# Attention scores of a head in two segments, three and two PSUM banks, instead of three

## The chip, the cores and the metric

The kernel runs on one core of a Trainium2 chip. The metric is the device time of one launch in microseconds (us). The kernel before takes 3364.94 us, the median of three runs (3364.42 to 3366.22).

## The reference, cut to what matters

The reference is one step of a backbone whose layer has attention, retention and routed experts. The change touches the attention alone:

```python
def block_attention(q, k, v):          # 2048 latent tokens in blocks of 128, 8 query heads, 2 key/value heads
    ...
    def one_block(qblk):
        s = jnp.einsum('bkgqd,bskd->bkgqs', qblk, k).astype(jnp.float32) * scale
        p = jax.nn.softmax(s, axis=-1).astype(v.dtype)
        return jnp.einsum('bkgqs,bskd->bkgqd', p, v)
```

A latent query sees 2048 latent keys and 128 cached context keys, 2176 keys or 17 key tiles of 128. The 128 new context tokens see only their own 128 keys. A head has 64 dimensions.

## The kernel before, in words

The stage `attention` runs over query tiles i = 0 to 16 (NT = 16): sixteen latent tiles, then one of context tokens. A tile has 8 heads h, and each head is one step. Tiles 2 to 14 are one hardware loop; the 8 steps of a tile are written out in it.

The work of a step is software-pipelined over heads. In step h TensorE (PE) turns the probabilities of head h (`turn`, L1292: transposes of 128x128 blocks with the identity, 4 in one PSUM bank; turns 0 to 3 have 4 blocks, turn 4 has one), multiplies values for the pair of heads before (`value`, L1310), and computes the scores of head h + 2 (`scores`, L1282). ScalarE (ACT) takes the exponentials of head h + 1 (`exp`, L1419, which also sums its outputs and reads that sum out) and keeps the high part of each turned bank (`turn`, L1427). VectorE (DVE) takes the maxima over the scores of head h + 2 (`scores`, L1502), combines them and scales them (L1506, L1512: `nm`, the bias of the exponential), keeps the low part of each turned bank (`turn`, L1529) and so frees the bank, and sums and inverts the totals (`total`, L1519, L1521).

The scores of a head fill five PSUM banks, `ps_s`; of these there is one set. So each segment of scores of head h + 2 waits until the exponential of the same segment of head h + 1 has read it: `pe.wait_ge(exped[seg], n)` in `scores`. The first turn of a head waits until its last exponential is done. The turns go through two further banks, `ps_t`, in rotation with the folds of a value pair (`fold`, L1322, every even step), the turned queries (`q`, L1263, at the head of step 6), the turned outputs (`out`, L1343, behind step 3) and a piece of a modulation vector (`mod`, L1331, in the place of the fold in steps 5 and 7).

Each engine executes its instructions in the order of the program, and that order is written by hand, one list for each engine: `PE_STEP`, `ACT_STEP`, `DVE_STEP`. `BANK_W` holds the columns of each score bank, `SEGS` the (first bank, banks) of each segment, `SEG_ORDER` the order of the segments. Before, segment 0 is 2 banks of 448 columns, segment 1 the same, segment 2 one bank of 384. The context tile has one segment of 128 columns and only turn 4.

Of the kernel before, what the change touches and what calls it, by code (L numbers as in the profile page):

```python
# [6 lines left out]
P = 128  # L7
# [3 lines left out]
NT = T_LAT // P  # L11
# [4 lines left out]
NQ = 8  # L16
# [29 lines left out]
AX = mybir.AxisListType.X  # L46
# [500 lines left out]
def retention(nc, g, a, s):  # L547

    with ExitStack() as ctx:
# [364 lines left out]
        def _(pe):  # L914
# [95 lines left out]

KEY_TILES = NT + 1

BANK_W = [448, 448, 448, 448, KEY_TILES * P - 4 * 448]
SEGS = [(0, 2), (2, 2), (4, 1)]
CTX_KEYS = NT + 1


PE_STEP = [("turn", 0), ("turn", 1), ("value", 0), ("value", 1), ("turn", 2), ("turn", 3), ("scores", 0), ("value", 2),
           ("scores", 2), ("turn", 4), ("fold", 0), ("scores", 1)]
ACT_STEP = [("keep", 0), ("turn", 0), ("turn", 1), ("exp", 0), ("exp", 2), ("turn", 2), ("turn", 3), ("exp", 1),  # L1020
            ("turn", 4)]
DVE_STEP = [("turn", 0), ("turn", 1), ("total", 0), ("turn", 2), ("turn", 3), ("scores", 0), ("turn", 4), ("scores", 2),
            ("fold", 0), ("scores", 1)]
SEG_ORDER = [0, 2, 1]
PIECES = [(0, 3), (3, 6), (6, 9), (9, 12), (12, 15), (15, KEY_TILES)]
GROUP = 2
NGRP = NQ // GROUP
# [2 lines left out]
def attention(nc, g, a, s):  # L1030


    with ExitStack() as ctx:
        k = Core(nc, ctx)
# [14 lines left out]
        fold = k.sb("a_fold", [P, HD])  # L1049
        o_sum = k.sb("a_o_sum", [P, GROUP, P])  # L1050
        att = k.sb("a_att", [P, NQ, HD])
        mx, nm = k.sb("a_mx", [P, 2, 4]), k.sb("a_nm", [P, 2])
        sums, total_s, rsum = k.sb("a_sums", [P, 2, 3]), k.sb("a_total", [P, 2]), k.sb("a_rsum", [P, NQ])
        attT = k.sb("a_attT", [P, 4, P])
        HALF = P // 2
        wm = [k.sb(f"a_wm{i}", [P, DC, w]) for i, w in enumerate((P, HALF))]
# [1 line left out]
        ps_s = k.ps("a_ps_s", [P, 5, 512])  # L1058
# [3 lines left out]
        kv_in, k_hi_ok, k_lo_ok, vals_ok = k.sems("a_kv_in", 2), k.sem("a_k_hi_ok"), k.sem("a_k_lo_ok"), k.sem("a_vals_ok")  # L1062
        k_turned, k_kept = k.sem("a_k_turned"), k.sem("a_k_kept")
        q_in, q_hi_ok, q_lo_ok = k.sem("a_q_in"), k.sem("a_q_hi_ok"), k.sem("a_q_lo_ok")
        scored, exped = k.sems("a_scored", 3), k.sems("a_exped", 3)
        max_ok, max_all, nmax_ok = k.sem("a_max_ok"), k.sem("a_max_all"), k.sem("a_nmax_ok")
        sum_ok, rsum_ok, hi_kept = k.sem("a_sum_ok"), k.sem("a_rsum_ok"), k.sem("a_hi_kept")
        filled, emptied = k.sems("a_filled", 2), k.sems("a_emptied", 2)
# [8 lines left out]
        block = blocks.enter_context(nc.Block())  # L1077

        def segs_of(i):
            return [2] if isinstance(i, int) and i == NT else SEG_ORDER  # L1080

        def turns_of(i):
            return [4] if isinstance(i, int) and i == NT else [0, 1, 2, 3, 4]

        def seg_scores(seg, w=None):
            b, m = SEGS[seg]
            return ps_s[:, b:b + m, 0:w or BANK_W[b]]

        def seg_probs(i, h, seg):
            b, m = SEGS[seg]  # L1090
            if isinstance(i, int) and i == NT:
                return prob[h % 2][:, (KEY_TILES - 1) * P:].rearrange("p (b w) -> p b w", b=1)
            at = sum(BANK_W[0:b])
            return prob[h % 2][:, at:at + m * BANK_W[b]].rearrange("p (b w) -> p b w", b=m)

        def seg_width(i, seg):
            return P if isinstance(i, int) and i == NT else BANK_W[SEGS[seg][0]]

# [138 lines left out]
        def _(pe):  # L1237
# [30 lines left out]
            def scores(i, h, seg, q_uses):  # L1268

                n = i * NQ + h  # L1270
                ctx_tile = isinstance(i, int) and i == NT
                if seg == segs_of(i)[0] and h == 0:
                    for b in range(2):
                        pe.wait_ge(emptied[b], q_uses[b])
                if not (isinstance(n, int) and n == 0):
                    pe.wait_ge(exped[seg], n)
                first, m = SEGS[seg]
                for b in range(first, first + m):
                    w = seg_width(i, seg)
                    src = CTX_KEYS * P if ctx_tile else sum(BANK_W[0:b])  # L1280
                    for part in range(2):
                        ins = nc.tensor.matmul(ps_s[:, b, 0:w], qT[:, h, :], keys[:, part, h // QPK, src:src + w],  # L1282
                                               start=(part == 0), stop=(part == 1))
                ins.then_inc(scored[seg], 1)
# [65 lines left out]
            for h in range(2):  # L1350
                for seg in SEG_ORDER:
                    scores(0, h, seg, [1, 1])
# [32 lines left out]
        def _(act):  # L1385
# [19 lines left out]
            def queries_hi(i):  # L1405
                act.wait_ge(q_in, (i + 1) * 16)
                if not (isinstance(i, int) and i == 0):

                    act.wait_ge(scored[2], (i - 1) * NQ + 1)
                nc.scalar.activation(q_parts[:, :, 0, :], q_row[:, :, :], ACT.Copy).then_inc(q_hi_ok, 1)  # L1410

            def exps(i, h, seg):

                n = i * NQ + h
                if seg == segs_of(i)[0]:
                    act.wait_ge(nmax_ok, n + 1)
                    if not (isinstance(n, int) and n < 2):
                        act.wait_ge(sum_ok, n - 1)
                nc.scalar.activation(seg_probs(i, h, seg), seg_scores(seg, seg_width(i, seg)), ACT.Exp,  # L1419
                                     bias=nm[:, h % 2:h % 2 + 1], scale=scale,  # L1420
                                     accum_out=sums[:, h % 2, seg:seg + 1]).then_inc(exped[seg], 1)

            def leave(i, h, kind, n, b, before):
                if kind == "turn":
                    act.wait_ge(filled[b], before + 1)
                    out = pT_hi[h // 2 % 2][:, 4 * n:min(4 * n + 4, KEY_TILES), h % 2, :]
                    nc.scalar.activation(out, ps_t[b][:, 0:out.shape[1], :], ACT.Copy).then_inc(hi_kept, 1)  # L1427
                elif kind == "q":
                    act.wait_ge(filled[b], before + 1)
                    nc.scalar.activation(qT[:, n * 4:n * 4 + 4, :], ps_t[b][:, :, :], ACT.Copy).then_inc(emptied[b], 1)  # L1430
                elif kind == "out":
                    act.wait_ge(filled[b], before + 1)
                    if n == 0 and not (isinstance(i, int) and i == 1):
                        act.wait_ge(att_out, (i - 1) * 16)
                    nc.scalar.activation(attT[:, 2 * n:2 * n + 2, :], ps_t[b][:, 0:2, :], ACT.Copy).then_inc(emptied[b], 1)

            def keep_sums(t, grp):
                act.wait_ge(valued, group_index(t, grp) + 1)
                nc.scalar.activation(o_sum[:, :, :], ps_o[:, :, :], ACT.Copy).then_inc(o_kept, 1)

            queries_hi(0)
            start = Bank(-1)
            for half_at in range(2):
                leave(0, 0, "q", half_at, *start.next())
            for seg in SEG_ORDER:
                exps(0, 0, seg)

            def body(i):
                last_tile = isinstance(i, int) and i == NT
                bank = Bank(i)  # L1450
                for h in range(NQ):
                    bank_of = bank.step(i, h)
                    for kind, n in step_events(i, h, ACT_STEP):
                        if kind == "exp":
# [19 lines left out]
        def _(dve):  # L1474
# [23 lines left out]
            def maxima(i, h, seg):  # L1498

                n = i * NQ + h  # L1500
                dve.wait_ge(scored[seg], n + 1)
                nc.vector.tensor_reduce(mx[:, h % 2, seg:seg + 1], seg_scores(seg, seg_width(i, seg)), AXY, ALU.max)\  # L1502
                    .then_inc(max_ok, 1)
                if seg == segs_of(i)[-1]:
                    dve.wait_ge(max_ok, (n + 1) * 3 if not (isinstance(i, int) and i == NT) else NT * NQ * 3 + h + 1)
                    nc.vector.reduce_max(mx[:, h % 2, 3:4], mx[:, h % 2, min(segs_of(i)):3], AX).then_inc(max_all, 1)  # L1506
                    dve.wait_ge(max_all, n + 1)
                    if not (isinstance(n, int) and n < 2):
                        dve.wait_ge(exped[SEG_ORDER[-1]], min(n - 1, NT * NQ) if isinstance(n, int) else n - 1)
                        if isinstance(n, int) and n - 1 > NT * NQ:  # L1510
                            dve.wait_ge(exped[2], n - 1)
                    nc.vector.tensor_scalar(nm[:, h % 2:h % 2 + 1], mx[:, h % 2, 3:4], -scale, None, ALU.mult)\  # L1512
                        .then_inc(nmax_ok, 1)

            def total(i, h):

                n = i * NQ + h
                dve.wait_ge(exped[segs_of(i)[-1]], n + 1)
                nc.vector.reduce_sum(total_s[:, h % 2:h % 2 + 1], sums[:, h % 2, min(segs_of(i)):3], AX).then_inc(sum_ok, 1)  # L1519
                dve.wait_ge(sum_ok, n + 1)  # L1520
                nc.vector.reciprocal(rsum[:, h:h + 1], total_s[:, h % 2:h % 2 + 1]).then_inc(rsum_ok, 1)  # L1521

# [54 lines left out]
            def body(i):  # L1577
                last_tile = isinstance(i, int) and i == NT
                bank = Bank(i)
                for h in range(NQ):  # L1580
                    if h == NQ - 3 and not last_tile:
                        queries_lo(i + 1)
                    bank_of = bank.step(i, h)
                    for kind, n in step_events(i, h, DVE_STEP):
                        if kind == "scores":
# [12 lines left out]
            for h in range(2):  # L1598
                for seg in SEG_ORDER:
                    maxima(0, h, seg)  # L1600
# [1079 lines left out]
```

## Time and profile before

| | |
|---|---|
| time, median of 3 | 3364.94 us |
| time of the profiled execution | 3365.65 us |
| its span, first to last instruction | 3363.9 us |
| PE busy | 3113.8 us, 93% |
| DVE busy | 1856.7 us, 55% |
| ACT busy | 1718.7 us, 51% |
| mean granted TensorE clock | 0.959 of 2.4 GHz |
| DMA | 394.61 MB, mean 117 GB/s |

The span is cut by stages that follow each other: projection, retention, attention, output projection, selection, experts. The attention's steps run from about 707 to 1663 us. Busy time of PE is modelled to the end of each matmul, so matmuls in a row overlap in it; what a matmul takes of PE's time is read from start to start.

### The profile page before, as it was taken

To read this page: it belongs to the slowest core of one execution; us is meant where nothing else is said; L and a number is where in the kernel's file an instruction comes from. 1 tells how busy PE (TensorE), PEld (TensorE's weight loads), DVE (VectorE), ACT (ScalarE), POOL (GpSimd) and SP (SyncE) were. 2 spreads that over 40 slices of the span, in tenths; PEclk is the share of its full clock that TensorE was granted. 3 is DMA by queue.
4 is the path that set the end of the run, shared out by engine and by line. 5 is a ranking of instruction groups with operands and counts; after the bars stand their busy time and mean duration, and the time that the engine had idled before them with its cause. 6 is when DMAs were issued, how large, how long until landed. Compare 5 with 4: busy or idle time off the path is not lost. (4 is left out here: it accounts for less than half of the span.)

```text
span 3363.9 us, 59296 instructions
## 1 busy us (share of the span) xinstructions
PE 3113.8 (93%) x21600; PEld 2851.6 (85%) x21600; DVE 1856.7 (55%) x3219; ACT 1718.7 (51%) x3389; POOL 412.5 (12%) x392
## 2 busy tenths in 40 slices
PE   6999997779999999999799856999999999999995
PEld 6888886668888888888688756999999999999995
DVE  2222224768888888888543394545544554554555
ACT  2222222567777777777533334455554455455454
POOL 0333333500000000000000000111111111111103
PEclk9999998879999999999899957999999999999998
DMA  6121114420000000000154305566665566666656
GB/s 231 47 81 63 63 63 149 138 91 23 19 28 19 22 22 25 22 21 26 42 182 151 111 1 194 185 190 190 187 189 184 181 188 189 183 187 189 186 173 258
DMA packets 316108, 394.61 MB, mean 117 GB/s; under 512 B 30356, under 2 KB 272232, under 8 KB 315000
## 3 DMA queue, kind: packets, MB, share of 16 engines
q1 hardware_dynamic: 304312, 347.30, 31.2%
q0 software_dynamic: 10560, 36.77, 4.8%
q10 hardware_dynamic: 1152, 9.44, 0.7%
q8 instruction: 51, 0.84, 0.1%
q14 instruction: 33, 0.27, 0.0%
HBM read 319.54 MB, written 74.06 MB: 117 GB/s over the span
## 5 line engine op out<-in xcount | busy, mean ns | idle before, releaser
L2522 DVE TENSOR_TENSOR e_w_lo<-e_raw,e_w_hi 128x2048 fp32r<-128x2048 f32 x192 | 440.2, 2292 | 486.8 <-ACT e_w_hi L2452 486.8
L93 PE MATMUL e_ps<-e_x_hi,e_w_hi 128*128 128x272 f32 x2048 | 601.9, 294 | 5.5 <-issue 5.5
L95 PE MATMUL e_ps<-e_x_hi,e_w_lo 128*128 128x272 f32 x2048 | 593.6, 290 | 0.0
L94 PE MATMUL e_ps<-e_x_lo,e_w_hi 128*128 128x272 f32 x2048 | 589.8, 288 | 0.0
L1529 DVE TENSOR_TENSOR a_pT_lo<-a_ps_t,a_pT_hi 128x512 fp32r<-128x512 f32 (+1 forms) x648 | 368.4, 602 | 137.3 <-ACT a_pT_hi L1427 137.0
L1427 ACT ACTIVATE a_pT_hi<-a_ps_t 128x512 fp32r<-128x512 f32 (+1 forms) x648 | 319.3, 532 | 171.2 <-PE a_ps_t L1292 166.5
L93 PEld LDWEIGHTS e_ps<-e_x_hi,e_w_hi 128*128 128x128 f32 x2048 | 386.1, 189 | 7.1 <-issue 5.5
L94 PEld LDWEIGHTS e_ps<-e_x_lo,e_w_hi 128*128 128x128 f32 x2048 | 386.8, 189 | 0.0
L95 PEld LDWEIGHTS e_ps<-e_x_hi,e_w_lo 128*128 128x128 f32 x2048 | 385.8, 188 | 0.0
L2452 ACT ACTIVATE e_w_hi<-e_raw 128x2048 fp32r<-128x2048 f32 x192 | 366.1, 1907 | 14.6 <-DMA e_raw<-in_w_gate 10.2
L1502 DVE TENSOR_REDUCE a_mx<-a_ps_s 128x1 f32<-128x896 f32 (+2 forms) x392 | 347.1, 893 | 26.8 <-PE a_ps_s L1282 26.8
L1292 PE MATMUL a_ps_t<-ident,a_prob 128*128 128x128 f32 x2184 | 329.4, 280 | 27.8 <-DVE a_pT_lo L1529 17.7
L1282 PE MATMUL a_ps_s<-a_keys,a_qT 128*128 128x448 f32 (+2 forms) x1296 | 342.3, 379 | 8.7 <-ACT a_prob L1419 6.4
L1419 ACT ACTIVATE a_prob<-a_ps_s,a_nm 128x896 f32<-128x896 f32 (+2 forms) x392 | 334.9, 859 | 19.2 <-DVE a_nm L1512 16.8
L1292 PEld LDWEIGHTS a_ps_t<-ident,a_prob 128*128 128x128 f32 x2184 | 244.9, 141 | 81.3 <-DVE a_pT_lo L1529 49.5
L93 PE MATMUL e_ps<-e_h_hi,e_w_hi 128*128 128x272 f32 x1024 | 298.2, 291 | 0.8 <-DVE e_h_lo L2578 0.8
L95 PE MATMUL e_ps<-e_h_hi,e_w_lo 128*128 128x272 f32 x1024 | 296.3, 289 | 0.0
L94 PE MATMUL e_ps<-e_h_lo,e_w_hi 128*128 128x272 f32 x1024 | 294.8, 288 | 0.0
L1310 PE MATMUL a_ps_o<-a_pT_hi,a_vals 128*128 128x256 f32 x1092 | 283.0, 293 | 2.6 <-DVE a_pT_lo L1529 1.5
L1310 PE MATMUL a_ps_o<-a_pT_lo,a_vals 128*128 128x256 f32 x1092 | 271.7, 282 | 0.0
L93 PE MATMUL p_psP<-w_in_hi,p_hhi 128*128 128x512 f32 (+1 forms) x680 | 254.7, 375 | 12.1 <-DVE p_hlo L441 12.1
L95 PE MATMUL p_psP<-w_in_hi,p_hlo 128*128 128x512 f32 (+1 forms) x680 | 255.1, 375 | 0.0
(307 smaller groups left out, 5430.1 us busy)
## 6 DMA issues: line engine op xcount, KB each, us to landing
e_raw<-in_w_gate SPq DMA_DIRECT2D x64, 1024.0 KB, 5.0
e_raw<-in_w_up SPq DMA_DIRECT2D x64, 1024.0 KB, 5.0
e_raw<-in_w_down SPq DMA_DIRECT2D x64, 1024.0 KB, 5.0
s_ret<-p_pr SPq DMA_DIRECT2D x17, 768.0 KB, 3.6
m_raw<-in_w_in ACTq DMA_DIRECT2D x8, 1152.0 KB, 7.2
o_cT<-s_ct SPq DMA_DIRECT2D x17, 512.0 KB, 4.8
s_x<-o_x SPq DMA_DIRECT2D x17, 512.0 KB, 5.0
s_xn<-o_xn SPq DMA_DIRECT2D x17, 512.0 KB, 3.5
```

The source lines that it names most:

```text
L93: nc.tensor.matmul(out, w_hi, x_hi, start=first, stop=False)
L94: nc.tensor.matmul(out, w_hi, x_lo, start=False, stop=False)
L95: return nc.tensor.matmul(out, w_lo, x_hi, start=False, stop=last)
L1282: ins = nc.tensor.matmul(ps_s[:, b, 0:w], qT[:, h, :], keys[:, part, h // QPK, src:src + w], start=(part == 0), stop=(part == 1))
L1292: ins = nc.tensor.transpose(ps_t[b][:, c % 4, :], prob[h % 2][:, c * P:(c + 1) * P], g["ident"][:, :])
L1310: ins = nc.tensor.matmul(ps_o[:, :, :], vals[:, src, grp * GROUP // QPK, :, :].rearrange("p d f -> p (d f)"), part[grp % 2][:, c, :, :], s ...
L1419: nc.scalar.activation(seg_probs(i, h, seg), seg_scores(seg, seg_width(i, seg)), ACT.Exp, bias=nm[:, h % 2:h % 2 + 1], scale=scale, accum_ ...
L1427: nc.scalar.activation(out, ps_t[b][:, 0:out.shape[1], :], ACT.Copy).then_inc(hi_kept, 1)
L1502: nc.vector.tensor_reduce(mx[:, h % 2, seg:seg + 1], seg_scores(seg, seg_width(i, seg)), AXY, ALU.max)\
L1529: nc.vector.tensor_tensor(pT_lo[h // 2 % 2][:, out, h % 2, :], ps_t[b][:, 0:m, :], pT_hi[h // 2 % 2][:, out, h % 2, :].bitcast(F32), ALU.s ...
L2452: nc.scalar.activation(w_hi[n % RING][:, :, :], raw[n % RING][:, :, :], ACT.Copy).then_inc(w_hi_ok, 1)
L2522: nc.vector.tensor_tensor(w_lo[n % RING][:, :, :], raw[n % RING][:, :, :], w_hi[n % RING][:, :, :].bitcast(F32), ALU.subtract).then_inc(w_ ...
```

## The change

A head's scores go in two segments: segment 0 is three banks of 448 columns, segment 1 two banks of 416. The lists of the three engines lose the third segment. On ACT, the high part of turn 4 also moves ahead of the last exponential; on PE and DVE turn 4 keeps its place ahead of the last scores. In the context tile the one segment is now the last one in the lists, behind turn 4.

```diff
-BANK_W = [448, 448, 448, 448, KEY_TILES * P - 4 * 448]
-SEGS = [(0, 2), (2, 2), (4, 1)]
+BANK_W = [448, 448, 448, 416, 416]
+SEGS = [(0, 3), (3, 2)]
+NSEG = len(SEGS)
...
 PE_STEP = [("turn", 0), ("turn", 1), ("value", 0), ("value", 1), ("turn", 2), ("turn", 3), ("scores", 0), ("value", 2),
-           ("scores", 2), ("turn", 4), ("fold", 0), ("scores", 1)]
-ACT_STEP = [("keep", 0), ("turn", 0), ("turn", 1), ("exp", 0), ("exp", 2), ("turn", 2), ("turn", 3), ("exp", 1),
-            ("turn", 4)]
-DVE_STEP = [("turn", 0), ("turn", 1), ("total", 0), ("turn", 2), ("turn", 3), ("scores", 0), ("turn", 4), ("scores", 2),
+           ("turn", 4), ("fold", 0), ("scores", 1)]
+ACT_STEP = [("keep", 0), ("turn", 0), ("turn", 1), ("exp", 0), ("turn", 2), ("turn", 3), ("turn", 4), ("exp", 1)]
+DVE_STEP = [("turn", 0), ("turn", 1), ("total", 0), ("turn", 2), ("turn", 3), ("scores", 0), ("turn", 4),
             ("fold", 0), ("scores", 1)]
-SEG_ORDER = [0, 2, 1]
+SEG_ORDER = [0, 1]
...
-            return [2] if isinstance(i, int) and i == NT else SEG_ORDER
+            return [NSEG - 1] if isinstance(i, int) and i == NT else SEG_ORDER
```

The rest of the diff sizes the tiles and semaphores by NSEG, adjusts the counts that are waited for (two maxima per head instead of three, the last segment's semaphore throughout), and lets the context tile use one bank of its two-bank segment.

## Rows read from the trace of the kernel before

**Rows 1.** A stretch: length, busy PE, PEld, DVE, ACT, POOL, clock, DMA share, GB/s.

```profile
760.00:1600.00 840.00, 815.56 (x5938) 733.95 (x5937) 690.18 (x1486) 625.32 (x1397) 0.00 (x0) 1.00 0.08 23
```

**Rows 2.** Waits in 760:1600: who waited for whom, us, times, longest.

```profile
PEld a_ps_t L1292 <- DVE a_pT_lo L1529: 40.5, 142, 0.7
PEld a_ps_s L1282 <- ACT a_prob L1419: 10.2, 29, 0.4
```

**Rows 3.** Timeline of PE, one step (h = 1): start us, us, engine, line.

```profile
1066.45 1.05 PE L1282 MATMUL a_ps_s<-a_keys,a_qT 128*128 128x448 f32 x4
...
1070.72 1.06 PE L1282 MATMUL a_ps_s<-a_keys,a_qT 128*128 128x448 f32 x4
1071.61 0.28 PE L1310 MATMUL a_ps_o<-a_pT_hi,a_vals 128*128 128x256 f32 x1
...
1072.09 0.52 PE L1282 MATMUL a_ps_s<-a_keys,a_qT 128*128 128x384 f32 x2
1072.44 0.27 PE L1292 MATMUL a_ps_t<-ident,a_prob 128*128 128x128 f32 x1
1072.79 1.08 PE L1282 MATMUL a_ps_s<-a_keys,a_qT 128*128 128x448 f32 x4
```

**Rows 4.** Timeline of ACT at the end of the same step.

```profile
1071.62 1.03 ACT L1419 ACTIVATE a_prob<-a_ps_s,a_nm 128x896 f32<-128x896 f32 x1
1072.51 0.23 ACT L1419 ACTIVATION_READ_ACCUMULATOR a_prob<-a_ps_s,a_nm 128x1 f32 x1
1072.75 0.28 ACT L1427 ACTIVATE a_pT_hi<-a_ps_t 128x128 fp32r<-128x128 f32 x1
1072.92 0.38 ACT L1439 ACTIVATE a_o_sum<-a_ps_o 128x256 f32<-128x256 f32 x1
```

**Rows 5.** Operations by form in 760:1600: count, busy us, mean ns, idle before.

```profile
L1502 DVE TENSOR_REDUCE a_mx<-a_ps_s 128x1 f32<-128x896 f32 x232 | 251.5, 1084 | 16.7 <-PE a_ps_s L1282 16.7
L1502 DVE TENSOR_REDUCE a_mx<-a_ps_s 128x1 f32<-128x384 f32 x116 | 63.8, 550 | 0.0
...
L1419 ACT ACTIVATE a_prob<-a_ps_s,a_nm 128x896 f32<-128x896 f32 x231 | 234.9, 1017 | 8.5 <-DVE a_nm L1512 6.3
...
L1419 ACT ACTIVATE a_prob<-a_ps_s,a_nm 128x384 f32<-128x384 f32 x115 | 66.1, 575 | 0.0
```

**Rows 6.** Timeline of PE, ends of steps 0, 4, 5 and 7 of a tile.

```profile
1065.97 0.27 PE L1292 MATMUL a_ps_t<-ident,a_prob 128*128 128x128 f32 x1
...
1034.86 0.27 PE L1292 MATMUL a_ps_t<-ident,a_prob 128*128 128x128 f32 x1
...
1035.46 0.85 PE L1282 MATMUL a_ps_s<-a_keys,a_qT 128*128 128x448 f32 x3
...
1042.13 0.27 PE L1292 MATMUL a_ps_t<-ident,a_prob 128*128 128x128 f32 x1
...
1043.95 0.85 PE L1282 MATMUL a_ps_s<-a_keys,a_qT 128*128 128x448 f32 x3
...
1058.03 0.27 PE L1292 MATMUL a_ps_t<-ident,a_prob 128*128 128x128 f32 x1
...
1059.32 0.47 PE L1282 MATMUL a_ps_s<-a_keys,a_qT 128*128 128x448 f32 x1
```

**Rows 7.** Timeline of DVE in the step of Rows 3: the bias.

```profile
1068.85 0.15 DVE L1512 TENSOR_SCALAR a_nm<-a_mx 128x1 f32<-128x1 f32 x1
```

**Rows 8.** Timeline of DVE: the same instruction of one tile and the next.

```profile
1003.33 0.15 DVE L1512 TENSOR_SCALAR a_nm<-a_mx 128x1 f32<-128x1 f32 x1
...
1061.76 0.15 DVE L1512 TENSOR_SCALAR a_nm<-a_mx 128x1 f32<-128x1 f32 x1
```

**Rows 9.** Busy time and granted clock, early and late in the context tile.

```profile
1640.00:1650.00 10.00, 7.74 (x69) 7.01 (x68) 4.48 (x22) 2.99 (x12) 0.00 (x0) 1.00 0.01 2
1652.00:1664.00 12.00, 7.98 (x31) 6.47 (x32) 4.36 (x24) 4.24 (x16) 0.00 (x0) 0.50 0.06 22
```

**Rows 10.** Timeline of PE: scores late in the context tile.

```profile
1658.72 0.69 PE L1282 MATMUL a_ps_s<-a_keys,a_qT 128*128 128x128 f32 x2 [1.01 <-ACT a_prob L1419]
```

More of the change, by code:

```diff
@@ L1052, in attention @@
         mx, nm = k.sb("a_mx", [P, 2, 4]), k.sb("a_nm", [P, 2])
-        sums, total_s, rsum = k.sb("a_sums", [P, 2, 3]), k.sb("a_total", [P, 2]), k.sb("a_rsum", [P, NQ])
+        sums, total_s, rsum = k.sb("a_sums", [P, 2, NSEG]), k.sb("a_total", [P, 2]), k.sb("a_rsum", [P, NQ])
         attT = k.sb("a_attT", [P, 4, P])
@@ L1064, in attention @@
         q_in, q_hi_ok, q_lo_ok = k.sem("a_q_in"), k.sem("a_q_hi_ok"), k.sem("a_q_lo_ok")
-        scored, exped = k.sems("a_scored", 3), k.sems("a_exped", 3)
+        scored, exped = k.sems("a_scored", NSEG), k.sems("a_exped", NSEG)
         max_ok, max_all, nmax_ok = k.sem("a_max_ok"), k.sem("a_max_all"), k.sem("a_nmax_ok")
@@ L1086, in seg_scores @@
             b, m = SEGS[seg]
-            return ps_s[:, b:b + m, 0:w or BANK_W[b]]
+            return ps_s[:, b:b + (1 if w == P else m), 0:w or BANK_W[b]]
         def seg_probs(i, h, seg):
@@ L1277, in scores @@
                 first, m = SEGS[seg]
-                for b in range(first, first + m):
+                for b in range(first, first + (1 if ctx_tile else m)):
                     w = seg_width(i, seg)
@@ L1407, in queries_hi @@
                 if not (isinstance(i, int) and i == 0):
-                    act.wait_ge(scored[2], (i - 1) * NQ + 1)
+                    act.wait_ge(scored[NSEG - 1], (i - 1) * NQ + 1)
                 nc.scalar.activation(q_parts[:, :, 0, :], q_row[:, :, :], ACT.Copy).then_inc(q_hi_ok, 1)
@@ L1504, in maxima @@
                 if seg == segs_of(i)[-1]:
-                    dve.wait_ge(max_ok, (n + 1) * 3 if not (isinstance(i, int) and i == NT) else NT * NQ * 3 + h + 1)
-                    nc.vector.reduce_max(mx[:, h % 2, 3:4], mx[:, h % 2, min(segs_of(i)):3], AX).then_inc(max_all, 1)
+                    dve.wait_ge(max_ok, (n + 1) * NSEG if not (isinstance(i, int) and i == NT) else NT * NQ * NSEG + h + 1)
+                    nc.vector.reduce_max(mx[:, h % 2, 3:4], mx[:, h % 2, min(segs_of(i)):NSEG], AX).then_inc(max_all, 1)
                     dve.wait_ge(max_all, n + 1)
                     if not (isinstance(n, int) and n < 2):
-                        dve.wait_ge(exped[SEG_ORDER[-1]], min(n - 1, NT * NQ) if isinstance(n, int) else n - 1)
-                        if isinstance(n, int) and n - 1 > NT * NQ:
-                            dve.wait_ge(exped[2], n - 1)
+                        dve.wait_ge(exped[NSEG - 1], n - 1)
                     nc.vector.tensor_scalar(nm[:, h % 2:h % 2 + 1], mx[:, h % 2, 3:4], -scale, None, ALU.mult)\
@@ L1518, in total @@
                 dve.wait_ge(exped[segs_of(i)[-1]], n + 1)
-                nc.vector.reduce_sum(total_s[:, h % 2:h % 2 + 1], sums[:, h % 2, min(segs_of(i)):3], AX).then_inc(sum_ok, 1)
+                nc.vector.reduce_sum(total_s[:, h % 2:h % 2 + 1], sums[:, h % 2, min(segs_of(i)):NSEG], AX).then_inc(sum_ok, 1)
                 dve.wait_ge(sum_ok, n + 1)
```

## Prediction

> **What bounds the kernel now.** The change touches attention alone, so I read the busy times of each engine there first, then the waits, then the timeline of one step. In 840 us of attention PE is busy 815.56 us, DVE 690.18 and ACT 625.32, the granted clock is 1.00 and the DMA share 0.08 [rows 1]: PE is the bound, no transfer is. Its waits in that stretch are small: weight loads wait 40.5 us on DVE's low parts and 10.2 us on ACT's exponentials, some 51 us or 6% [rows 2]. ACT has 215 us to spare [rows 1]. The order of attention is the same in each tile: one instruction of one tile and the next lie 1061.76 - 1003.33 = 58.43 us apart [rows 8], 8 steps of 7.30 us.
>
> The reader should see how a step ends. In the step of h = 1, PE starts the 448-column scores of the last segment at 1066.45 and again at 1072.79 [rows 3]: 6.34 us. Near the end it does segment 0's scores, 4 value matmuls, segment 2's scores, turn 4 (start 1072.44), and the last scores 0.35 us later [rows 3]. These last scores overwrite the banks that ACT's last exponential reads. That exponential ran at 1071.62 to 1072.65 and its sum was read out until 1072.74 [rows 4]; PE started 0.05 us later. It ran while PE did scores, values and scores: PE's own work was its cover. ACT took turn 4 after it, at 1072.75 [rows 4].
>
> **The change, part by part.**
>
> *1. ACT takes turn 4 ahead of the last exponential.* This is the term that decides. ACT's turn 4 needs PE's turn 4, which comes behind scores and values; the last exponential now stands behind it; and PE's last scores wait for that exponential, as does the next head's first turn, queued behind them. What was parallel becomes a chain, from the start of PE's turn 4 (T4) to the start of the last scores (S1):
> - PE turn 4 to ACT's start: 1072.44 to 1072.75 = 0.31 [rows 3, 4]. There ACT may still have been just busy, and the matmul itself lasts 0.27, so 0.31 is near its least.
> - ACT turn 4 to its next operation: 1072.92 - 1072.75 = 0.17 [rows 4].
> - the exponential of 2 x 416 = 832 columns. A 896-column one takes 1.12 from its start to the end of the read of its sum (1071.62 to 1072.74 [rows 4]). Slope: (1017 - 575)/512 = 0.86 ns a column [rows 5], so 64 fewer save 0.055: 1.07.
> - end of that read to PE: 0.05 [rows 3, 4].
>
> Sum 1.60 us. Before, T4 to S1 took: odd step without extra 0.35 [rows 3] and 0.29 in step 3; even steps, with a fold between, 1066.45 - 1065.97 = 0.48 [rows 3, 6], the same in step 2 to 0.01, and 0.60 in step 4 [rows 6], about the same in step 6; step 5, with the large modulation piece, 1.82; step 7, with the small one, 1.29 [rows 6]. The fold and the pieces stand between turn 4 and the last scores still, so they fill the hole and don't add to it; in step 5 the piece is longer than the chain and hides it. Added: steps 1 and 3, 1.25 + 1.31; steps 0, 2, 4, 6, 1.12 + 1.12 + 1.00 + 1.04; step 5, 0; step 7, 0.31. Together 7.15 us a tile.
>
> *2. Three segments become two.* The columns stay 2176. PE: 10 matmuls as before. Segment 0 of six matmuls: four take 1071.61 - 1070.72 = 0.89, two more at 448/2.4 = 187 ns each give 1.26, against 0.89 + 0.35 (1072.09 to 1072.44) = 1.24 before [rows 3]. +0.02. The last scores have 128 columns fewer over four matmuls, -0.05. DVE: one maximum less; slope (1084 - 550)/512 = 1.04 ns, so 1.55 + 1.02 against 2 x 1.08 + 0.55: -0.15. ACT: one exponential and one read less, 0.24 by the same intercept and about 0.1 [rows 5]. What of this is on the path? The low parts of turns 0 and 1 give back the banks for turns 2 and 3 (the 40.5 us of [rows 2]), and they stand behind the last maximum and the bias (1068.85 [rows 7]); the scores of segment 0 follow turn 3. That leg, from the last scores' start at 1066.45 to 1070.72 [rows 3], gets shorter by 0.05 (scores) + 0.065 (maximum of 832) = 0.11. In every second plain step DVE comes late to the last maximum, from the operation now gone; its 0.15 [rows 5] goes there too, once or twice a tile. So -0.11 x 8 - 0.15, and +0.02 x 8: about -0.8 us a tile (0.87). It could be nothing, if ACT's now longer first exponential takes its place, or up to -0.15 a step, -1.2.
>
> *3. The longer first exponential.* PE's scores of segment 0 wait for all three banks: from the bias (1068.85 + 0.15 [rows 7]) the exponential and its read take 1.12 + 0.385 = 1.5, so about 3.9 to 4.1 us after the last scores started, against 4.27 for their start before (1070.72 - 1066.45) and 4.2 now. The cover is 0.1 us thin; were it gone, 0.1 us a step, +13 us in all. I take nothing. The 1.55 us maximum of segment 0 delays DVE's low part of turn 4 by some 1 us; the bank is needed only behind the stall, so this costs nothing as long as the stall is there.
>
> *4. Edges.* The last latent tile has one such step less (the exponential of step 7 there is of the context tile). In the context tile the order is turned round as well: the small scores come behind turn 4 and the fold. Late in it PE waits 1.01 us on the exponential at 1658.72 [rows 10]; a DVE low part leaves that loop, so I take -3 us, with 0 to -5 as bounds, and +1 for the change from latent to context.
>
> Sum: 7.15 - 0.8 = 6.35 us a tile; 15 tiles 95, the last 5, context -2: +98 us. On the profiled execution's 3365.65 us that is 3464; it stands 0.7 us above the median of the runs, so 3463. Nothing outside attention depends on it but by its end.
>
> **A rule weighed.** ACT and DVE pay a fixed part per instruction here: by the intercepts, 575 - 384 x 0.86 = 245 ns for an exponential, 150 ns for a maximum [rows 5]. The Trainium skill, Perfetto Trace Analysis, section Optimizing Scalar/DVE Operations, says that grouping into larger operations can improve throughput if the engine is saturated, and that where these engines are not saturated but cause bubbles on others, breaking instructions up may let work finish sooner. The trace agrees with the second half: ACT at 625 of 840 us is not saturated. By the first half alone the sum would be a gain, my third rival; by the second a loss.
>
> **The rivals.**
> - *A. The stall takes the place of waits that exist.* PE idles more at the end of a step, DVE and ACT catch up, and the 51 us of waits [rows 2] go. Over all 935 us of steps they are 57: +98 - 57, 3406. For it: DVE has 0.15 us less a step. Against: turns 2 and 3 wait for low parts that stand behind the last maximum, and this starts only after the last scores; the stall moves it along, so the wait stays.
> - *B. The clock falls.* PE would be idle about 1.2 us in a step of 8.1; the busy share drops from 97% to some 87%. Early in the context tile it is 77% at clock 1.00, later 67% at 0.50 [rows 9]. At 87% I expect 1.00. If half the 128 steps ran at the lower level, 6.6 us of PE work each would be doubled: +420, 3885.
> - *C. Faster.* If the engines beside PE set the pace, the two operations saved would decide: place, the end of DVE's and ACT's work in a step; price, 128 x 0.15 to 128 x 0.24 = 19 to 31 us, 3340. It decides from the point where the last exponential is done before PE comes to the last scores, which asks that turn 4 be ready more than 1.2 us before PE reaches it. The order allows that only in step 5.
> - *D. No change,* if PE's turn 4 were ready early through some cover that I don't see: 3365.
>
> **How the numbers follow.** Forecast 0.84, A 0.08, B 0.03, C 0.03, D 0.02. The forecast's own range: a stall of 1.5 to 1.7 us instead of 1.60 is 12 us either way over 112 steps that pay; term 2 from 0 to -1.2 a tile is +13 to -6; term 3 to +13; edges 3. Together 3440 to 3488. I give 3436 to 3490, which leaves out the rivals. A measurement of this kernel tells 0.2% (7 us) from no change. Faster C 0.03, same D 0.02, slower 0.95.
>
> **What would show it.** In the profile after: ACT's last exponential directly behind its turn 4, and ACT's wait ahead of turn 4 grown to about 1.2 us; PE's weight load of the last scores waiting on the exponential some 1.1 to 1.3 us in seven of eight steps, none in step 5; the same instruction one tile apart 64.8 us instead of 58.43; PE busy near 87% at clock 1.00; maxima of 1.55 and 1.02 us. The forecast is wrong if the tiles lie under 62 us apart, if the last scores start less than 1.5 us after turn 4, or if the clock leaves 1.00.

## The result, and the profile after

The changed kernel takes 3462.74 us (median of 4 runs, 3461.32 to 3465.64) beside 3364.86 us for the kernel before. The ratio is 1.0289, 95% interval 1.0276 to 1.0301: 98 us slower, where 98 were forecast (3463 us, range 3436 to 3490). Its span is 3459.7 us, 95.8 more than before.

The same stretch of attention as in [rows 1], in the changed kernel:

```profile
760.00:1600.00 840.00, 737.80 (x5366) 677.50 (x5366) 622.43 (x1237) 540.00 (x1056) 0.00 (x0) 1.00 0.07 20
```

PE's busy share fell from 97% to 88% at an unchanged clock of 1.00. DVE and ACT fell as well, 690 to 622 and 625 to 540 us, since 840 us now hold 104 steps instead of 115. Per step PE is busy 7.09 us in both kernels: nobody works longer, all wait. Who waits is in the view of waits for that stretch; it answers to [rows 2]:

```profile
PE a_ps_s L1282 <- ACT a_prob L1419: 84.7, 91, 1.3
...
PEld a_ps_s L1282 <- ACT a_prob L1419: 98.9, 91, 1.5
PEld a_ps_t L1292 <- DVE a_pT_lo L1527: 30.4, 113, 1.0
...
DVE a_mx L1502 <- PE a_ps_s L1282: 107.3, 104, 1.2
...
ACT a_pT_hi L1427 <- PE a_ps_t L1292: 257.7, 219, 1.6
```

The wait of PE's weight loads on the exponential grew from 10.2 to 98.9 us: 91 times 1.09 us, in 91 of the 104 steps of that stretch, seven of eight. In PE's own idle time it is 84.7 us, 6.5 us for each of the stretch's 13 tiles. The wait on DVE's low parts fell from 40.5 to 30.4. The step of h = 1 again, PE first, with the end of the step before it (answers to [rows 3, 6]); the columns are start, length, engine, line, and in brackets the idle time and its releaser (a row of last scores with x1 is the first of its four matmuls, at which the view ends):

```profile
1037.33 0.27 PE L1292 MATMUL a_ps_t<-ident,a_prob 128*128 128x128 f32 x1
1037.44 0.56 PE L1322 MATMUL a_ps_t<-a_fold,a_o_sum 128*128 128x64 f32 x4
1038.90 0.46 PE L1282 MATMUL a_ps_s<-a_keys,a_qT 128*128 128x416 f32 x1 [0.91 <-ACT a_prob L1419]
...
1043.09 1.45 PE L1282 MATMUL a_ps_s<-a_keys,a_qT 128*128 128x448 f32 x6
1044.86 0.27 PE L1292 MATMUL a_ps_t<-ident,a_prob 128*128 128x128 f32 x1
1046.43 0.45 PE L1282 MATMUL a_ps_s<-a_keys,a_qT 128*128 128x416 f32 x1 [1.30 <-ACT a_prob L1419]
```

and ACT in the same step (answers to [rows 4]):

```profile
1042.86 1.11 ACT L1427 ACTIVATE a_pT_hi<-a_ps_t 128x512 fp32r<-128x512 f32 x2
1045.16 0.28 ACT L1427 ACTIVATE a_pT_hi<-a_ps_t 128x128 fp32r<-128x128 f32 x1 [1.20 <-PE a_ps_t L1292]
1045.34 0.95 ACT L1419 ACTIVATE a_prob<-a_ps_s,a_nm 128x832 f32<-128x832 f32 x1
1046.17 0.20 ACT L1419 ACTIVATION_READ_ACCUMULATOR a_prob<-a_ps_s,a_nm 128x1 f32 x1
```

The reader can follow the chain across the two: PE turn 4 at 1044.86, ACT's high part at 1045.16 after 1.20 us in which ACT had nothing that its order let it do, the exponential at 1045.34, its sum read out at 1046.37, PE's last scores at 1046.43. From turn 4 to the last scores it is 1.57 us where it was 0.35 [rows 3]. With a fold between, 1037.33 to 1038.90, it is 1.57 as well: the fold fills part of the hole, and the idle time is 0.91 instead of 1.30.

In steps 5 and 7 a modulation piece stands in the place of the fold. The timeline of PE at the end of a step 7 and of a step 5:

```profile
1029.17 0.27 PE L1292 MATMUL a_ps_t<-ident,a_prob 128*128 128x128 f32 x1
1029.37 1.09 PE L1331 MATMUL a_ps_t<-cc,a_wm 128*64 128x2 f32 x16
1030.74 0.46 PE L1282 MATMUL a_ps_s<-a_keys,a_qT 128*128 128x416 f32 x1 [0.28 <-ACT a_prob L1419]
...
1076.97 0.27 PE L1292 MATMUL a_ps_t<-ident,a_prob 128*128 128x128 f32 x1
1077.08 1.85 PE L1331 MATMUL a_ps_t<-cc,a_wm 128*128 128x2 f32 x16
1078.78 0.43 PE L1282 MATMUL a_ps_s<-a_keys,a_qT 128*128 128x416 f32 x1
```

In step 7 the chain is 1.57 us again and shows by 0.28 us; in step 5 the piece is longer (1.81 from turn 4 to the scores, 1.82 before) and PE waits for nothing.

The instruction of [rows 8] in the changed kernel, one tile and the next, on DVE's timeline:

```profile
1033.06 0.15 DVE L1510 TENSOR_SCALAR a_nm<-a_mx 128x1 f32<-128x1 f32 x1
...
1097.64 0.16 DVE L1510 TENSOR_SCALAR a_nm<-a_mx 128x1 f32<-128x1 f32 x1
```

64.58 us against 58.43. The other tiles between the third and the fifteenth lie 64.5 to 64.7 us apart.

### The profile page after: what moved, and what is told of

It reads as the page before. It is cut to its first block and busy times, and to the rows that moved or that the text cites. A ratio compares the mean times of both kernels' runs of the same rounds, so it can differ in the third digit from the quotient of the medians.

```text
span 3459.7 us, 58910 instructions
## 1 busy us (share of the span) xinstructions
PE 3116.3 (90%) x21600; PEld 2870.9 (83%) x21600; DVE 1856.6 (54%) x3091; ACT 1685.7 (49%) x3133; POOL 412.8 (12%) x392
## 5 line engine op out<-in xcount | busy, mean ns | idle before, releaser
L1282 PE MATMUL a_ps_s<-a_keys,a_qT 128*128 128x448 f32 (+2 forms) x1296 | 325.3, 381 | 111.2 <-ACT a_prob L1419 110.0
L1502 DVE TENSOR_REDUCE a_mx<-a_ps_s 128x1 f32<-128x1344 f32 (+2 forms) x264 | 331.5, 1256 | 142.7 <-PE a_ps_s L1282 142.7
L1282 PEld LDWEIGHTS a_ps_s<-a_keys,a_qT 128*128 128x128 f32 x1296 | 226.8, 191 | 139.6 <-ACT a_prob L1419 129.4
L1419 ACT ACTIVATE a_prob<-a_ps_s,a_nm 128x1344 f32<-128x1344 f32 (+2 forms) x264 | 301.2, 1141 | 6.0 <-DVE a_nm L1510 4.8
```

## The experiments

Each was timed together with the kernel before on one chip; the ratios are to that time, 3364.8 to 3365.8 us.

**1. Two segments, without the turned bank's move.** The changed kernel, one line of it back.

```diff
-ACT_STEP = [..., ("exp", 0), ("turn", 2), ("turn", 3), ("turn", 4), ("exp", 1)]
+ACT_STEP = [..., ("exp", 0), ("turn", 2), ("turn", 3), ("exp", 1), ("turn", 4)]
```

> The changed kernel with ACT's last exponential back ahead of its turn 4; two segments as in the change. Theory (the loss is the chain PE turn 4, ACT turn 4, last exponential, PE last scores): the chain is gone, so the time falls by nearly all of the 98 us. What two segments alone do is two terms: 0.11 us less ahead of turn 3, and against it DVE's maximum over three banks (1.55 us) ahead of its low part of turn 4, which has no stall to hide in now. 3352 to 3375 us, 3358 likeliest; tiles 57.6 to 59 us apart; PE waits on the exponential under 0.3 us a step. Rival (the longer first exponential and maximum are what costs): it stays slow, 3400 us or more, with PE waiting ahead of the scores of segment 0.

Measured: 3352.91 us, ratio to the kernel before 0.9966 (0.9955 to 0.9977). The whole loss is gone and 12 us more. Tiles lie 57.9 us apart. ACT on its timeline, in an odd step, and PE's last scores in the same step:

```profile
1067.43 0.95 ACT L1419 ACTIVATE a_prob<-a_ps_s,a_nm 128x832 f32<-128x832 f32 x1
1068.26 0.20 ACT L1419 ACTIVATION_READ_ACCUMULATOR a_prob<-a_ps_s,a_nm 128x1 f32 x1
1068.73 0.28 ACT L1427 ACTIVATE a_pT_hi<-a_ps_t 128x128 fp32r<-128x128 f32 x1 [0.27 <-PE a_ps_t L1292]
```

```profile
1068.43 0.27 PE L1292 MATMUL a_ps_t<-ident,a_prob 128*128 128x128 f32 x1
1068.52 1.02 PE L1282 MATMUL a_ps_s<-a_keys,a_qT 128*128 128x416 f32 x4
```

The exponential starts a microsecond before PE's turn 4 and its sum is read out by 1068.46; PE starts 0.06 us later, and the view of waits has no wait of the scores on an exponential in the whole stretch. The two segments are not what costs.

**2. The move alone.** The kernel before with its three segments.

```diff
-ACT_STEP = [..., ("exp", 0), ("exp", 2), ("turn", 2), ("turn", 3), ("exp", 1), ("turn", 4)]
+ACT_STEP = [..., ("exp", 0), ("exp", 2), ("turn", 2), ("turn", 3), ("turn", 4), ("exp", 1)]
```

> The kernel before with its three segments, and ACT's turn 4 moved ahead of the last exponential, nothing else. Theory: the whole loss and a bit more, since the last exponential has 896 columns: 0.31 + 0.17 + 1.12 + 0.05 = 1.65 us from turn 4 to the last scores; +7.5 us a tile less some 0.3 that DVE gives back, +113 us: 3478 us; tiles 65.5 us apart. Rival (the segments cost): under 3400 us.

Measured: 3474.62 us, ratio 1.0327 (1.0309 to 1.0344): 110 us slower from one item in one list. Its view of waits shows the same line as the changed kernel, a little larger, as the last exponential has 896 columns:

```profile
PEld a_ps_s L1282 <- ACT a_prob L1419: 102.4, 91, 1.7
```

With experiment 1 the sum closes: the move alone +110, two segments alone -12, both +98. Some 3 of the 110 us are the clock's in the profiled execution: the tiles lie 65.2 us apart but for two of 66.8 and 66.7, and in each of these the granted clock fell for a while. One of the two places, among the windows of that stretch (the clock is 0.57):

```profile
1263.00:1267.00 4.00, 3.97 (x21) 3.97 (x22) 2.31 (x7) 3.23 (x8) 0.00 (x0) 0.57 0.17 66
```

**3. More cover.** The changed kernel with PE's turn 4 ahead of the last value group.

```diff
-PE_STEP = [..., ("scores", 0), ("value", 2), ("turn", 4), ("fold", 0), ("scores", 1)]
+PE_STEP = [..., ("scores", 0), ("turn", 4), ("value", 2), ("fold", 0), ("scores", 1)]
```

> The changed kernel with PE's turn 4 ahead of the step's last value group instead of behind it: a dose of cover. Theory: the chain stays 1.60 us but starts 0.48 us (odd steps) or 0.72 us (even steps) of PE work earlier, so each step that stalls gets shorter by that, step 5 not, step 7 by 0.3: -4.1 us a tile, 3396 us, tiles 60.5 us apart. Rival (the stall only stands in for something else, DVE's low parts): no more than 20 us less, 3440 or more.

Measured: 3394.62 us, ratio 1.0092 (1.0075 to 1.0109), 68 us less than the changed kernel; the tiles lie 60.5 us apart, as expected. The wait on the exponential halves in the same stretch:

```profile
PEld a_ps_s L1282 <- ACT a_prob L1419: 47.6, 84, 1.0
```

**4. A shorter link.** The changed kernel with other bank widths.

```diff
-BANK_W = [448, 448, 448, 416, 416]
+BANK_W = [512, 512, 512, 320, 320]
```

> The changed kernel with three banks of 512 columns and two of 320: the last exponential has 640 columns instead of 832, the first 1536 instead of 1344. Theory: 192 x 0.86 = 0.165 us less in the chain of each step that stalls, and the last maximum and scores shorter by 0.20 and 0.16 us, of which some 0.15 us count before PE waits for the longer first exponential: -1.1 to -2.3 us a tile, 3426 to 3445 us. Rival (the first exponential's cover of 0.1 us is what matters): no gain or a loss, 3460 to 3480.

Measured: 3444.23 us, ratio 1.0238 (1.0221 to 1.0256), 18 us less than the changed kernel and at the upper end of what was expected. The first exponential's thin cover did give way: the waits of the scores on an exponential rose to 148 in number from 91, yet their total fell. The new ones stand ahead of segment 0's scores and are short, as the second row, from PE's timeline, shows:

```profile
PEld a_ps_s L1282 <- ACT a_prob L1419: 95.5, 148, 1.4
...
1037.39 1.23 PEld L1282 LDWEIGHTS a_ps_s<-a_keys,a_qT 128*128 128x128 f32 x6 [0.17 <-ACT a_prob L1419]
```

**5. Less cover.** The changed kernel with the fold, or the modulation piece that stands in its place, ahead of turn 4.

```diff
-PE_STEP = [..., ("value", 2), ("turn", 4), ("fold", 0), ("scores", 1)]
+PE_STEP = [..., ("value", 2), ("fold", 0), ("turn", 4), ("scores", 1)]
```

> The changed kernel with PE's fold or modulation piece ahead of turn 4 instead of behind it: cover taken away from the chain. Theory (a chain of 1.60 us from PE's turn 4, nothing of PE's between): the folds' 0.37 to 0.43 us in even steps now add in full, +1.6 us a tile; in step 5 the piece of 1.7 us comes before the chain, +1.5; in step 7 the piece of 1.0 to 1.2, +1.1. Together +4.2 us a tile, +66: 3529 us, tiles 68.8 us apart. Rival (PE's stall is set by something that does not move with turn 4): within 10 us of 3463.

Measured: 3556.83 us, ratio 1.0567 (1.0549 to 1.0584): 94 us more than the changed kernel, in the direction of the theory but 28 us beyond it. The granted clock had moved. PE in a step 5 and behind it, then the windows around it, where the clock is the number behind the five busy times (1.00, 0.70, 0.87):

```profile
1245.75 1.84 PE L1331 MATMUL a_ps_t<-cc,a_wm 128*128 128x2 f32 x16
1247.45 0.31 PE L1292 MATMUL a_ps_t<-ident,a_prob 128*128 128x128 f32 x1
1249.06 1.30 PE L1282 MATMUL a_ps_s<-a_keys,a_qT 128*128 128x416 f32 x4 [1.30 <-ACT a_prob L1419]
1250.15 1.91 PE L1263 MATMUL a_ps_t<-ident,a_q_parts 128*128 128x128 f32 x8
```

```profile
1244.00:1248.00 4.00, 3.76 (x30) 3.48 (x27) 2.75 (x3) 1.06 (x4) 0.00 (x0) 1.00 0.00 0
1248.00:1252.00 4.00, 2.94 (x13) 2.58 (x14) 1.75 (x5) 1.61 (x4) 0.00 (x0) 0.70 0.45 131
1252.00:1256.00 4.00, 4.00 (x31) 3.85 (x31) 1.52 (x4) 3.82 (x8) 0.00 (x0) 0.87 0.00 0
```

The modulation piece is 16 matmuls of 2 columns, 1.7 us in which the timeline shows PE busy; behind it PE stood idle for 1.30 us. Then the clock was at its lower level, 1.2 GHz, for a while, and the eight turned queries took 1.91 us instead of 1.03. Such drops come again through the whole of attention, behind some steps 5 and 7 and not behind others, and the mean clock of the stretch 760 to 1600 is 0.97. Tiles lie 68.9 and 71.1 us apart in turns, where 68.8 was expected of both: the tiles of 68.9 have no drop and take what the theory says, those of 71.1 have two and take 2.2 us more. That is some 19 us over 16 tiles. The context tile's heads take 30.4 us at a mean clock of 0.61, instead of 23.7 at 0.79 in the changed kernel, another 7. How much of these 7 is the clock's was not separated; in experiment 8, which has the same order of folds there, they take 24.4.

**6. The candidate of experiment 1 with an early turn 4 on PE,** experiments 1 and 3 together.

> The kernel with two segments and ACT's last exponential ahead of turn 4 (3353 us), with PE's turn 4 ahead of the last value group as in the run before with 3395 us. Theory: what turn 4's place was worth (68 us there) came from the chain alone; here ACT takes turn 4 behind its last exponential, which ends at about the end of the values, so nothing follows: 3350 to 3358 us. Rival (an early turn 4 helps by itself, by freeing its bank): 3340 or less.

Measured: 3352.38 us, ratio 0.9959 (0.9945 to 0.9973), no different from experiment 1 (their intervals overlap). Turn 4's place on PE, worth 68 us with the chain, is worth nothing without it.

**7. Wider banks in the candidate,** experiments 1 and 4 together.

> A candidate for the fastest: two segments, the last exponential ahead of turn 4, and banks of 512 x 3 and 320 x 2. No chain that 192 columns less could shorten. The last scores and maximum are 0.16 and 0.20 us shorter, but DVE's maximum over 1536 columns takes 1.75 us, and its low part of turn 4 and last maximum stand behind it: DVE becomes late by 0.2 to 0.6 us at the end of a step. Estimate 3345 to 3375 us, 3360 likeliest, so no gain over 3353. A rival by which the shorter last segment helps as it did in the changed kernel (18 us): 3335.

Measured: 3384.5 us, ratio 1.0055 (1.0038 to 1.0072), 9.5 us above the top of the expected range: a miss. The mechanism is the one named, but its price was too low and it was not the only one. Tiles lie 59.8 us apart, 1.9 more than in experiment 1. DVE and then PE at the end of an odd step:

```profile
1081.18 1.76 DVE L1502 TENSOR_REDUCE a_mx<-a_ps_s 128x1 f32<-128x1536 f32 x1
1082.86 0.28 DVE L1527 TENSOR_TENSOR a_pT_lo<-a_ps_t,a_pT_hi 128x128 fp32r<-128x128 f32 x1
```

```profile
1082.16 0.60 PE L1292 MATMUL a_ps_t<-ident,a_prob 128*128 128x128 f32 x4
1083.19 0.66 PE L1292 MATMUL a_ps_t<-ident,a_prob 128*128 128x128 f32 x4 [0.43 <-DVE a_pT_lo L1527]
```

The longer maximum holds back DVE's low part of turn 4 and with it a turned bank, for which the next head's second turn then waits 0.43 us. Over 760 to 1600, against experiment 1, PE's idle time ahead of turns rose from 8.1 to 18.9 us, that ahead of the turned outputs, also on a low part, from 8.0 to 13.5. The weight loads of segment 0's scores now wait on the first exponential too, 57 times and 10.9 us, where in experiment 1 they did not. Together these are 27 us in 14 tiles, which is the 1.9 us a tile. The expected time had nothing for the last of the three.

**8. The clock, by itself.** Experiment 5 with the modulation pieces behind turn 4 again, the folds still ahead of it.

```diff
                 order = [("mod", MOD_STEPS.index(h)) if kind == "fold" else (kind, n) for kind, n in order]
+                at = [kind for kind, n in order].index("mod") if order[0] == ("turn", 0) else 0
+                if order[at][0] == "mod" and order[at + 1] == ("turn", 4):
+                    order[at:at + 2] = order[at + 1], order[at]
```

> As the run with fold and modulation ahead of turn 4 (3557 us, 28 more than expected, with a clock of 0.949 and drops to the lower level all through attention), but the modulation pieces in steps 5 and 7 go behind turn 4 again; the folds stay ahead of it. Theory: the folds' 0.37 to 0.43 us in four even steps add in full, +1.6 us a tile, +26: 3489 us, and the clock stays 1.00 in attention, because the drops came from the piece and the stall in a row in steps 5 and 7. Rival (the missing 28 us and the drops come from the folds' new place or from the larger share of idle time in general): 3500 or more, or a clock under 1.00 in attention.

Measured: 3490.15 us, ratio 1.0369 (1.0352 to 1.0387). The stretch of attention:

```profile
760.00:1600.00 840.00, 720.91 (x5227) 658.67 (x5225) 607.92 (x1206) 525.88 (x1026) 0.00 (x0) 1.00 0.07 20
```

The folds add what they should: tiles lie 66.2 us apart, 1.6 more than in the changed kernel. The clock's mean rounds to 1.00 with PE busy 86%, against 0.97 in experiment 5, so moving the pieces back removed the drops behind steps 5 and 7. It is not quite 1.00 throughout, though. One tile took 67.8 us, and in it the clock fell behind a step 3, where there is no piece. PE's timeline there and the window with the end of it (the clock is 0.70; the added lines move the line numbers by 3, so L1346 is the turned outputs and L1295 the turns):

```profile
1400.96 1.02 PE L1285 MATMUL a_ps_s<-a_keys,a_qT 128*128 128x416 f32 x4 [1.30 <-ACT a_prob L1422]
1401.82 0.60 PE L1346 MATMUL a_ps_t<-ident,a_att 128*128 128x128 f32 x4
1402.76 1.80 PE L1295 MATMUL a_ps_t<-ident,a_prob 128*128 128x128 f32 x8 [0.34 <-ACT a_attT L1438]
...
1404.00:1408.00 4.00, 4.00 (x26) 3.98 (x25) 1.65 (x5) 2.97 (x6) 0.00 (x0) 0.70 0.17 66
```

The eight turns took 1.80 us instead of 1.09. The two drops of experiment 2 stand at the same place, behind a stall of 1.36 us and a gap of 0.34. So the piece and the stall in a row brought most of the drops of experiment 5, and stalls without a piece brought a few as well; why these steps and not the same ones of other tiles is open.

## Why the prediction was right

**The chain (term 1)** was forecast at 1.60 us and measured 1.57 in steps with a fold, with nothing and with the small piece. Link by link: 0.30 to ACT (0.31 forecast), 0.18 to the exponential (0.17), 1.03 for the 832-column exponential and its read (1.07), 0.06 to PE (0.05). Experiments 1 and 2 show that it is the term that decides, and 3, 4 and 5 that it answers to its cover and its length: 68 us less where 66 were expected, 18 less where 18 to 37 were, and, in experiment 8, 27 more where 26 were (1.5 of the 27 are the tile with the drop).

**Which steps pay** was right: 91 of 104 waits, seven of eight steps, none in step 5, 0.28 us of idle time in step 7.

**Two segments (term 2)** were forecast to give back 0.8 us a tile. The tile grew by 64.58 - 58.43 = 6.15 us, where 7.15 - 0.8 = 6.35 was forecast. With a chain of 1.57 us the seven steps that pay add 6.94 instead of 7.15, which leaves -0.79 for this term in the changed kernel. Experiment 1 shows the two segments without the chain: -0.56 us a tile (57.87). There it is net of what DVE's longer maximum costs when no stall hides it; and the exponentials and maxima took 0.947, 1.383, 1.025 and 1.548 us, against 0.96, 1.40, 1.02 and 1.55 by the slopes.

**The longer first exponential (term 3)** cost nothing, as taken: the scores of segment 0 start 1043.09 - 1038.90 = 4.19 us after the last scores (4.2 forecast) and wait for no exponential in the changed kernel. That this cover was thin was right too: experiment 4's count of waits shows it gone with 192 columns more.

**The edges.** -2 us for the context tile and its border was forecast, with +1 of it for the border. Between the first and the last bias of the context heads it is 23.7 instead of 24.5 us, a gain of 0.8 where 3 were taken: this term was too large by a factor of three to four. The last latent tile grew by 6.0 us instead of 5. The first fifteen tiles grew by 92 us together instead of 95, since the first two grew by 5.5 and 6.0 only, which evens it out. That the sum is exact to a microsecond is luck; the chain and term 2 are right to some 3%, the edges are not.

**The range** was not added up rightly. Its own terms, all at their worst together, give 3442 to 3504 and not "3440 to 3488"; the 0.1 us of the stall over 112 steps is 11 us and not 12. The measured time lies inside either.

**The rivals.** *A* (the stall takes the place of the waits on DVE) fails: they fell from 40.5 to 30.4 us, per step from 0.35 to 0.29, not to nothing. *B* (the clock) did not happen in the changed kernel: the clock is 1.00 in the stretch 760 to 1600. By the letter of the prediction's sign ("if the clock leaves 1.00") there is one place to name, the border to the context tile, where it is 0.57 in 1740 to 1744, behind 10 us with PE busy 81%. B stood nearer than its chance of 0.03 says: experiment 5, with the same stall behind a piece of narrow matmuls, has the drops, some 19 us of its time in the latent tiles, and experiments 2 and 8 have a few. *C* (faster) is what experiment 1 shows, once the chain is away: -12 us, not the -19 to -31 priced for the case that DVE and ACT set the pace. *D* (no change, through some cover) fails: ACT had nothing to do for 1.20 us ahead of turn 4.

**The rule weighed.** The prediction read a loss out of the rule's second half, and that reading fails: two segments by themselves gained 12 us (experiment 1), and the whole loss came from the order of two operations. The Trainium skill, Perfetto Trace Analysis, section Optimizing Scalar/DVE Operations, speaks there of larger operations and of breaking instructions up, not of their order. Its first half is for a saturated engine; here the grouping gained with DVE busy 82% and ACT 74% of the stretch before. Its second half fits experiment 7, in which the longer operations cost 32 us against experiment 1, since they hold back work that PE waits for.

The fastest version found is that of experiments 1 and 6: 3353 us, 12 us under the kernel before.

## What to carry to other kernels

An in-order engine with time to spare can still be given an order that costs its time: before an operation is moved ahead of another on such an engine, look up what the moved one waits for, and who waits for the one that is passed. Here ACT was busy 74% and the passed exponential could run a microsecond before the other's operand was there; the loss was the whole chain behind the late operand, less whatever work the waiting engine has between its two ends. When a change has two parts, run each alone: one was worth -12 us and the other +110.

## What the runs showed of the hardware that was not expected

A run of 16 matmuls of 2 columns counts as busy time in the timeline, but in experiment 5, with 1.30 us of idle time behind it, the granted clock fell to its lower level again and again. With 1.30 us of idle time behind wide matmuls it stayed at 1.00 in all 13 tiles of the stretch in the changed kernel, fell once in experiment 8, and fell twice in experiment 2, where the idle time was 1.36 us. A drop cost 1.1 us in experiment 5 and 1.5 to 1.6 us in the other two. No experiment here separates what decides between the same steps of different tiles; a mean clock that prints as 1.00 over 840 us does not rule such a drop out, and the distance from tile to tile shows it.
